# Attention and mixture-of-experts block on one core: twelve places for expert weights, a first gather in two banks, and another order for the last two experts

## The reference

```
h = x + hybrid_mixer(rms_norm(x))
logits = rms_norm(h) @ w_router + b_router          # 256 x 32
gates = softmax(top_4(logits))
for each expert e, on the tokens that chose it:
    hgu = xb @ w_gu[e] + b_gu[e]                    # 1024 x 2048 weights
    gate = min(hgu[:, :1024], 7); up = clip(hgu[:, 1024:], -7, 7)
    act = (up + 1) * gate * sigmoid(1.702 * gate)
    y = act @ w_down[e] + b_down[e]                 # 1024 x 1024 weights
out = h + sum over the experts of gate * y
```

## Time and profile before

| | |
|---|---|
| median of 3 runs | 1159.17 us (1157.65 to 1160.5) |
| the profiled execution | 1161.69 us, its span 1159.9 us |
| TensorE (PE) busy | 1093.5 us, 94% of the span |
| VectorE, ScalarE busy | 260.5 us, 140.7 us |
| mean DMA rate | 376 GB/s, 435.66 MB in all |
| mean granted clock of TensorE | 0.993 |

### The profile page before, as it was taken

One profiled execution on the slowest core, in us unless ns is written; L12 is line 12 of the kernel. 1 busy time (PEld: TensorE's weight loads), 2 busy tenths in 40 slices (PEclk: granted clock), 3 DMA queues, 4 the chain that ended last, 5 costly groups with the idle time before them and its releaser, 6 DMA issues.

```text
span 1159.9 us, 11496 instructions
## 1 busy us (share of the span) xinstructions
PE 1093.5 (94%) x5084; PEld 472.4 (41%) x5084; DVE 260.5 (22%) x610; ACT 140.7 (12%) x242; POOL 9.8 (1%) x18
## 2 busy tenths in 40 slices
PE   7999999999999999999999989999999999999997
PEld 3676778543333333333333333333333333333332
DVE  1574322222221111111211111111111111111111
ACT  2315331001000000000000000000000000000000
POOL 1100000000000000000000000000000000000000
PEclk9999999989999999999999999999999999999999
DMA  9456534789999999999999999999999999999994
GB/s 271 150 207 229 193 142 174 294 336 425 429 427 429 427 427 427 428 428 428 427 428 427 429 425 428 427 428 427 427 427 427 428 428 427 429 427 429 428 426 204
DMA packets 44355, 435.66 MB, mean 376 GB/s; under 512 B 6192, under 2 KB 7376, under 8 KB 19632
## 3 DMA queue, kind: packets, MB, share of 16 engines
q1 hardware_dynamic: 43888, 434.29, 89.7%
q0 software_dynamic: 96, 0.08, 0.2%
q10 hardware_dynamic: 320, 0.53, 0.1%
HBM read 433.85 MB, written 1.05 MB: 375 GB/s over the span
## 4 chain that ended last, share of the span: by engine, by line
PE 59%; DMA 36%; DVE 2%; ACT 1%; issue 0%; another core or an unknown queue 0%; SPq 0%; ACTq 0%; DVEq 0%
PE Pp L750 20%; DMA ring<-in_w_gate_up 15%; DMA unit<-in_w_gate_up 12%; PE Bp L764 11%; DMA att_pair<-in_w_gate_up 8%; PE Pp L471 7%; PE Ap L778 4%; PE Bp L736 3%; PE Pp L459 3%; PE Pp L639 2%; PE Ap L650 2%; PE Pp L498 1%; PE Bp L757 1%; DVE G L1220 1%; DMA unit<-in_w_in 1%; PE Pp L698 1%
## 5 line engine op out<-in xcount | busy, mean ns | idle before, releaser
L750 PE MATMUL Pp<-ring,OBT 128*64 128x512 f32 x1120 | 253.7, 600 | 23.9 <-DMA ring<-in_w_gate_up 23.9
L1209 DVE TENSOR_SCALAR G<-Pp 128x512 f32<-128x512 f32 x32 | 22.1, 692 | 668.3 <-PE Pp L750 668.3
L750 PEld LDWEIGHTS Pp<-ring,OBT 128*64 128x64 f32 x1120 | 78.5, 138 | 186.6 <-issue 137.3
L764 PE MATMUL Bp<-ring,G 128*64 128x512 f32 x560 | 125.4, 595 | 2.3 <-DVE G L1220 1.1
L750 PE MATMUL Pp<-unit,OBT 128*64 128x512 f32 x352 | 79.7, 595 | 7.2 <-DMA unit<-in_w_gate_up 7.2
L471 PE MATMUL Pp<-norm_pair,unit 128*128 128x256 f32 x384 | 85.2, 380 | 0.0
L1408 ACT ACTIVATE G<-G 128x512 f32<-128x512 f32 x32 | 20.2, 630 | 503.7 <-DVE G L1209 503.7
L471 PEld LDWEIGHTS Pp<-norm_pair,unit 128*128 128x128 f32 x384 | 72.1, 190 | 10.9 <-issue 1.1
L764 PEld LDWEIGHTS Bp<-ring,G 128*64 128x64 f32 x560 | 38.7, 137 | 76.6 <-issue 70.4
L778 PE MATMUL Ap<-G,cst 64*128 64x512 f32 x264 | 65.6, 615 | 1.4 <-ACT G L1415 1.4
L736 PE MATMUL Bp<-X,cst 128*64 128x512 f32 x240 | 56.6, 593 | 0.0
(11 more groups left out here) (218 smaller groups left out, 840.1 us busy)
## 6 DMA issues: line engine op xcount, KB each, us to landing
ring<-in_w_gate_up SPq DMA_DIRECT2D x70, 2048.0 KB, 46.0
ring<-in_w_down SPq DMA_DIRECT2D x35, 2048.0 KB, 47.3
unit<-in_w_gate_up SPq DMA_DIRECT2D x22, 2048.0 KB, 46.2
more<-in_w_gate_up SPq DMA_DIRECT2D x12, 2048.0 KB, 46.1
unit<-in_w_down SPq DMA_DIRECT2D x12, 2048.0 KB, 44.8
att_pair<-in_w_gate_up SPq DMA_DIRECT2D x12, 2048.0 KB, 47.2
norm_pair<-in_w_gate_up SPq DMA_DIRECT2D x12, 2048.0 KB, 46.4
unit<-in_w_in SPq DMA_DIRECT2D x7, 2048.0 KB, 7.7
```

Of the source, the lines that this page charges most:

```text
L750: last = mm((Gps, Ups)[q // 2][64 * (q % 2):64 * (q % 2) + 64, :], xT[:, k % 4, k // 4, :], w[:, q * 512:(q + 1) * 512], start=False, stop ...
L764: last = mm(Yps[64 * hf:64 * hf + 64, :], hT[:, c, s, :], w[:, c * 1024 + hf * 512:][:, 0:512], start=s == 0 and c == 0, stop=s == DN - 1 ...
L1209: V.tensor_scalar(gm, Gps, LIMIT, None, ALU.min).then_inc(d_gm, 1)
```

## The change

The number of places goes from 11 to 12. The twelfth is the upper half of the old `G` and a region `once` beside it that holds what is used only before the experts: some constants, `KAT`, the router weights, the rank tables. `G` and `once` are one buffer `gate_rest` now, and the constants are loaded in two parts. The last two places of the first round, 10 and 11, are loaded in halves (`HALVED`): the first halves early, the second halves when the router and the rank products are done. The thirteenth piece, which goes back to place 0, is loaded in halves too: the first as soon as expert 0 has done its first k-step (`gu_first`).

The router's product is written 128 columns wide (`wide_router`; the further columns are not used). The zero matmuls are gone; the first scatter starts the banks. The first gather writes its two halves to different banks, with a semaphore each, and gate/up of expert 0 starts when the first half of `xT` is made.

The turns are taken from a list `use`. It is as before up to expert 29; then come gate/up of 30, gate/up of 31, down of 30, down of 31. `last_experts` writes that order out on TensorE and ScalarE; the gate/up and down sums of expert 31 use other banks and buffers (`Tps`, `Ups`, `gm_last`, `GT_last`). The last piece is loaded in two halves, and TensorE waits for each.

```diff
-PLACES = 11
+PLACES = 12
+HALVED = (10, 11)
...
+        use = [(e, i) for e in range(NE - 2) for i in range(TURNS)]
+        use += [(e, i) for e in (NE - 2, NE - 1) for i in range(GU)]
+        use += [(e, i) for e in (NE - 2, NE - 1) for i in range(GU, TURNS)]
...
             load(7)
+            sp.wait_ge(bias_ok, 2)
+            load_half(10, 0)
+            load_half(11, 0)
             sp.wait_ge(m_wo, 4)
             load(8)
             load(9)
-            sp.wait_ge(bias_ok, 2)
             sp.wait_ge(m_lr, TB)
-            load(10)
+            load_half(10, 1)
+            sp.wait_ge(m_rk, TB)
+            load_half(11, 1)
+
+            sp.wait_ge(gu_first, 1)
+            load_half(PLACES, 0)
+            released(PLACES)
+            load_half(PLACES, 1)
...
+            released(LAST)
+            load_half(LAST, 0, last_half)
+            load_half(LAST, 1)
...
-                    last = mm(Pp[:, 0, b * NE:(b + 1) * NE], XT[:, k, b * P:(b + 1) * P], WR[:, k, :],
+                    last = mm(Pp[:, 0, b * P:(b + 1) * P], XT[:, k, b * P:(b + 1) * P],
+                              wide_router[:, k * NE:k * NE + P],
...
-            pe.wait_ge(z_ok, 1)
-            for bank in range(4):
-                mm(Ap[:, bank, :], zero[:, 0:P], zero[:, P:], start=True, stop=False, skip_group_check=True)
             pe.wait_ge(bias_ok, 2)
             biases()
             pe.wait_ge(d_oh, 2)
-            gather_block(Tps, 1, 0, KC).then_inc(m_ga, 1)
+            gather_first(1, 0).then_inc(m_g0, 1)
+            pe.wait_ge(v_rk, 1)
+            gather_first(1, 1).then_inc(m_ga, 1)
...
+                gate_up_expert(e)
+                gather_expert(n)
+                scatter_expert(e - 1)
...
+                turn_act().then_inc(m_ht, 1)
+                gate_up_expert(n)
+                pe.wait_ge(d_ht, e + 1)
+                down(piece(turn_of[e, GU]), 0).then_inc(dn_used, 1)
...
+                turn_act(Tps).then_inc(m_ht, 1)
+                down(piece(turn_of[e, GU + 1]), 1).then_inc(m_y, 1)
+                pe.wait_ge(d_ht, n + 1)
+                down(piece(turn_of[n, GU]), 0, Ups, hT_last).then_inc(dn_used, 1)
+                scatter_expert(e)
+                pe.wait_ge(last_half, 16)
+                down(places[LAST % PLACES], 1, Ups, hT_last, 0, 2)
+                down(piece(LAST), 1, Ups, hT_last, 2, 4).then_inc(m_y, 1)
```

More of the change, by code:

```diff
@@ L355, in released, with load_half @@
                     sp.wait_ge(m_y, e0 + 1)
+            def load_half(turn, h, full=None):
+                e, i = use[turn]
+                src = gu_src(e, i) if i < GU else dn_src(e, i - GU)
+                part = slice(2048 * h, 2048 * h + 2048)
+                sp.dma_start(places[turn % PLACES][:, part], src[:, part])\
+                    .then_inc(full or place_full[turn % PLACES], 16)
             sp.wait_ge(v_pv, 2)
@@ L855, in expert @@
                     for b in range(TB):
-                        scatter(b)
+                        scatter(b, start=True)
                 elif e != BREAK:
@@ L868, in expert @@
                 for s in range(DN):
-                    last = down(piece(TURNS * e + GU + s), s)
+                    last = down(piece(turn_of[e, GU + s]), s)
                     last.then_inc(m_y if s == DN - 1 else dn_used, 1)
@@ L1272, in _ @@
             take_expert(BREAK)
-            for e in range(BREAK, NE):
+            for e in range(BREAK, NE - 2):
                 expert(e)
+            spread_expert(NE - 2)
+            select_expert(NE - 1)
+            swiglu_expert(NE - 2)
+            take_expert(NE - 1)
+            turned_expert(NE - 2)
+            spread_expert(NE - 1)
+            swiglu_expert(NE - 1, gm_last)
+            dve.wait_ge(m_ht, NE)
+            V.tensor_copy(gm_last, Tps).then_inc(d_ht, 1)
             for b in range(TB):
```

186 lines of the change are left out of this document (122 added, 64 removed).

## The result

| | before | after |
|---|---|---|
| median | 1158.41 us (4 runs, 1157.35 to 1160.5) | 1150.74 us (4 runs, 1150.55 to 1152.06) |
| profiled execution, span | 1161.69, 1159.9 us | 1150.55, 1148.7 us |
| TensorE busy | 1093.5 us | 1084.1 us |
| mean DMA rate | 376 GB/s | 379 GB/s |

The ratio of the medians is 0.9925, with a 95% interval of 0.9903 to 0.9948. The forecast was 1150.4 us, so the time came out as predicted. That the forecast time was hit within 0.4 us is partly luck, since the median of before came out 0.8 us lower than the one that the forecast started from.

What follows compares the result with a forecast made beforehand. The prediction took the experts to be bound by loading the weights. Its terms, 4.9 + 2.5 + 1.4 = 8.8 us, taken from the median 1159.17 gave 1150.4 us, own range 1148.9 to 1152.2, wider range 1146.5 to 1155.0.

Steps and rivals of the forecast that it cites:

- The early halves: Front, 225 to 237 us: two half loads issued early fill idle DMA time; 4.9 us gained, bounds 0 to 4.9.
- Rival (c): Front: early halves find no idle engines or are paid back; gain 3.9 us, 1155.3 us; chance 0.06.
- The second idle place: DMA idle stretch from 250 to 254 us: closes, 2.5 us gained, bounds 0 to 2.7.
- The tail: Last two experts: span ends 11.3 to 11.5 us after the last landing instead of 12.9; 1.4 us gained.
- (a): End of the kernel: TensorE stays at half clock until the output; slower, 1167 us; chance 0.04.
- (b): The idle place at 250 us stays, or the stream tears at 270; gain 6.3 or less, 1153 us; chance 0.12.
- (d): End: last landings even out and TensorE is ready for the last half; gain 11.4 us, 1147.8 us; chance 0.16.

Runs made afterwards that it cites:

- e1: Changed kernel with the first halves of the two last places loaded together with their second halves: 1158.07 us, ratio 0.998 to before.
- e4: Changed kernel with the last two experts in the old order and the last piece loaded whole: 1152.99 us, ratio 0.994 to before.
- e2: Changed kernel with both halves of the thirteenth piece waiting until the whole first piece is used: 1151.72 us, ratio 0.9928 to before.
- e5: Changed kernel with the scatter of expert 30 moved ahead of the third of the last four down pieces: 1151.54 us, ratio 0.9923 to before.
- e3: Changed kernel with the router product 32 columns wide again: 1151.43 us, ratio 0.9925 to before.
- e0: The changed kernel run once more without edits, as the control: 1151.5 us, ratio 0.9931 to before.
- e9: Changed kernel with 32-wide router product, four extra 512-wide matmuls, gate/up waiting for all of xT, thirteenth piece waiting for the whole first piece: 1151.88 us.
- e10: The kernel before with one edit, the ninth piece loaded early, during the output projection: 1159.48 us, ratio 0.9997 to before.
- e8: Changed kernel with the last piece loaded whole, new order of the last experts kept: 1152.92 us, ratio 0.9932 to before.
- e6: Changed kernel with the ninth piece loaded once the output projection is done with its part of the ring: 1149.24 us, ratio 0.9909 to before.
- e7: Changed kernel with the edits of e5 and e6 together: 1148.12 us, ratio 0.9895 to before.
- e11: The changed kernel run again without edits, as control on the chip of e7, e9 and e10: 1152.35 us, ratio 0.9927 to before.

## Why the prediction was right

**The early halves, 4.9 us.** They go at once (204.19 and 204.67) and their bytes flow in the idle stretch. Taking them back costs 5.4 us in the profiles and 6.6 in the medians (e1). The term was right, and a little small; what the rest of it is stays open. Rival (c), that they are paid back, is out.

**The second idle place, 2.5 us.** It closed, and the windows give its size in DMA time: 2.6 us lost before, 0.1 in e1, 0 after. At the end less of it is seen. The last landing is 913.1 us behind the projection before and 911.6 in e1, so 1.5 us earlier, and as the new order at the end makes the landing 0.4 later (e4), the idle place is worth 1.5 to 1.9 us there, against one profile of before. The size was nearly right.

The cause that the prediction put first was not: it counted on the first half of the thirteenth piece going at 246.8, and e2, without that half, loses nothing. The reason is the start of expert 0. The prediction kept the clock at 0.50 as in the earlier trace rows, and nine of the ten profiles with the wide product read 1.00 there (e5 did not). So expert 0 started 4.5 us earlier instead of 2.6, and the whole first piece was used 11.4 us behind the projection, while the queue lasts until 250.3 - 233.87 = 16.4 by the prediction's own sum. This part of the hit is luck: the clock did more than was asked. It was not needed, though. In e3, at half clock, the prediction's own times come true (start 9.5 us behind, half load 12.5 behind) and the whole piece is used at 246.1, 14.0 us behind, still ahead of 16.4.

The runs give the rule for this stretch. With the new front the release is in time at either clock (e0, e3). With nearly the old front at full clock it is in time as well (e9: 12.6 us). With the old front and half clock it comes at 17.4 (before) and 15.9 (e10), and the DMA engines stand still. So either the shorter front or the full clock is enough. Not shown is what the twelfth place is worth in itself: no run has eleven places and the rest of the change.

**The tail, 1.4 us.** L + 11.3 against L + 12.9 is 1.6 us, and the sequence was the predicted one, with waits before three down pieces and a scatter standing before the last. But against the old order with twelve places (e4) it is 1.1 us of tail, and 0.4 of it goes to a later landing: 0.6 net in the profiles, up to 1.6 in the medians. Of the 0.5 us between the tails of before and e4, 0.2 is the drop of the clock, which e4 didn't have. The halves of the last piece gave nothing in themselves in the profiles (e8). What the prediction named as the hindrance, the scatter and the third piece in front of the halves, is confirmed by e5: the scatter moved one place ahead gives 0.9 us.

One reading of the prediction is wrong here. It has TensorE wait for no weight after 1132.57 and prices the half clock there at 8.78 - 7.08 = 1.7 us. But by its own pitch the next gate/up piece landed only at 1137.3, and e4 shows the wait for it, 1.24 us. At half clock the longer first piece takes the place of that wait. So the drop cost 0.2 us before (against e4) and 0.5 in e8.

**The rivals.** (a), half clock to the end: no drop behind 1120 us in the profile after, though TensorE paused three times. The prediction tied this rival to the Trainium skill, page "TensorE: Matmul & The Clock Gate", section "HAM oscillation — how this bites in real kernels". That section tells of a loop that waits about 3 to 5 us for data at every tile and starts each next tile cold. The pauses of 1.08, 1.53 and 1.34 us are shorter, and each is followed by a piece of 3.65 us, so they don't contradict it; the prediction left the length of the waits out and so applied it too widely. What this case adds is that a drop can follow shorter pauses: e8 shows the one that occurred behind 1120 us in this order, behind 1.82 us, and it did not last. (b), a second idle place that stays: out. (d), an end better by 4 us since the last landings even out: out; the last landing came 7.0 us earlier and the rate still thins out at the end (151 GB/s from 1130 to 1138 us).

**Sum.** The gain of 8.6 us in the profiles divides into 7.0 at the last landing and 1.6 behind it. By runs, e1 lies 5.4 above the control and 3.0 below before, 1.5 of it at the landing and 1.5 in the tail (the control ends 0.2 later than the profile after). These are differences of the same spans, so that they add up proves nothing; the evidence for each term is its own run or window. In the medians the whole is 7.2 to 8.4 us.

## What to carry to other kernels

In a stream that the weights bind, a load that is issued earlier pays only if the next place comes free before the queue is dry. The same edit gave nothing in the median where the release came 15.9 us behind the projection and the queue was dry at 12 (e10), and 2.4 us where the release came at 9.7 (e6). Count a chain of waits against the time at which the queue runs dry, not against the old start, and then see which of several edits is needed: here the half load was not (e2), and the shorter front and the full clock each had cover from the other. When an engine ran at half clock and then met a wait, compare with a run at full clock before pricing the drop, since the wait may have swallowed it. Where single executions differ by the time of an early step, measure from an event behind it to the end; that told 0.9 us (e5) where the medians could not.

## What the runs showed of the hardware

- The first large product took 13.97 to 16.33 us (13.97 in after, e0, e3, e6, e7 and e10, 15.43 in e5, 15.67 in e11, 16.19 in e2, 16.33 before) with the same instructions, and the rest of the program moved along with it. Its cause isn't known. It explains up to 2.4 us between two executions.
- The length of a pause alone does not decide whether the granted clock falls. In the same part of the program, behind the same pause of 1.82 us, the piece took 3.65 us in e2 and 5.35 in e8; in the old order the clock stayed at 1.00 behind 2.40 us (e4) and fell behind 2.41 (e10) and 2.57 us (before). What else goes in stays open. TensorE in e2:
```profile
1130.18 3.65 PE L805 MATMUL Bp<-ring,gate_rest 128*64 128x512 f32 x16 [1.82 <-DMA ring<-in_w_down]
```
and in e10:
```profile
1129.40 8.78 PE L753 MATMUL Pp<-ring,OBT 128*64 128x512 f32 x32 [2.41 <-DMA ring<-in_w_gate_up]
```
- Half clock in the front (e3: 0.50 from 238 to 240 us, gate/up 1.8 us later) cost nothing at the end, since the DMA engines ran at 434 GB/s beside it.
